# Keys and values of the linear heads: transposed by VectorE blocks and DMA instead of TensorE, and a new order of steps inside each head

## The chip, the cores and the metric

One core of a Trainium2 chip runs the whole kernel. The metric is the device time of one execution in microseconds (us), the median of three runs; lower is better. TensorE (PE) multiplies, VectorE (DVE) and ScalarE (ACT) work elementwise and read PSUM, GpSimd (POOL) works elementwise on SBUF and issues DMAs, SyncE (SP) only issues DMAs. Each engine has its own queue of instructions, run in order; engines meet through semaphores alone.

## The reference, cut to what matters

One layer over 576 tokens (512 of a prompt, 64 of a running stream), width 2048. One input projection gives the operands of three mixers (pooling, stick-breaking attention with 8 heads of 128, linear "mLSTM" heads, 4 of 256), their gates and three merge gates of width 2048. The linear heads are the part that changes:

```python
s = jnp.einsum('bhld,bhsd->bhls', qc, kc) * w_intra
num = jnp.einsum('bhls,bhsv->bhlv', s, vc) + w_inter[..., None] * jnp.einsum('bhlk,bhkv->bhlv', qc, c)
den = jnp.sum(s, axis=-1) + w_inter * jnp.einsum('bhlk,bhk->bhl', qc, n)
h_out = num / jnp.maximum(jnp.abs(den), jnp.exp(-m_t))[..., None]
...
c_new = decay[..., None, None] * c + jnp.einsum('bhs,bhsk,bhsv->bhkv', w_end, kc, vc)
...
h_ml = h_ml * lax.rsqrt(jnp.mean(h_ml * h_ml, axis=-1, keepdims=True) + RMS_EPS)
...
for bi, yb in enumerate((pool_y, sb_y, ml_y)):
    gated = yb * jax.nn.silu(cols(OFF_Z + bi * BRANCH_W, BRANCH_W))
    term = jax.nn.sigmoid(cols(...)) * jnp.einsum('btw,wd->btd', gated, w_branch[bi])
    merged = term if merged is None else merged + term
y = jnp.einsum('btd,de->bte', merged, w_out)
```

Scores `s` contract over the channels of keys and queries; the weighing `num` and the state `c_new` contract over tokens, so for them keys and values must lie with tokens on the partitions.

## The kernel before, in words

Everything is computed in fp32 quality out of fp32r matmuls: each operand is split into a high and a low part (`..._hi` made by ACT, `..._lo` by DVE as the rest), and three products are added.

**Input projection** (0 to about 1577 us). 68 pairs of column tiles, each by seven products of Strassen-Winograd form (`pair_products`, L1029). Activations lie with channels on the partitions and tokens along the row. The list `SPILLS` sets which group of columns each pair from the 3rd on computes: queries, keys and values of the attention heads (SQ, SK, SV), those of the linear heads (MQ, MK, MV), gates (MO, ZSB, ZML, G0 to G2). POOL stores each pair to `z_scratch` in HBM (`store_pair`). Pairs of a kind "turned" (SK, SV: eight pairs) are also transposed: DVE transposes all 32x32 blocks of the pair into `tokens` (`to_tokens`, L2264), and 16 DMAs of POOL put the blocks in their places in HBM (`store_tokens`). Every turned pair is followed by one of another kind.

**Attention heads** (1577 to 1742 us). A "segment" `seg(h, s)` is half of a tile of the branch projection: 24 matmuls that need the weights `wb_hi`, `wb_lo` and gated activations `gt_hi`, `gt_lo`. Segments are the filler that PE runs while DVE and ACT work on a head. `SB_SLOTS` says how many segments stand behind each of the steps scores, (middle of the scores), `weights_to_keys` and `weigh_values` of a head. After a tile DVE merges it with its gate (`merge`, L2485 or L2488 and L2491).

**Linear heads** (1742 to 1921 us). `ML_SLOTS` is the same for `ml_head`. Its steps on PE are, in order: KTR, ten transposes of keys from `ml_k` to the PSUM tensor `M` (L1047); SCORES (L1368); VTR, ten transposes of values from `ml_v`; WEIGH, numerator and denominator (L1347, L1390); SSQ, sums of squares by a matmul with ones (L1396); STATE, the new state (L1407). All steps share the four banks of `M`, so each waits until DVE or ACT has read the step before. Between the steps stand 2, 1, 1, 2, 1, 1 segments. On DVE and ACT each head has: `mk_hi`, `mk_lo` (keys times a decay, split); `decay_rows` (five instructions into `W_ml`, L2602), the exponential on ACT (L1844), a causal mask on POOL (L2985, four instructions), the product with the scores (L2655), the split `S_hi`, `S_lo` and the split of values `mv_hi`, `mv_lo`; copies of the numerator (L2676 to L2680); squares, `den`, a reciprocal (L2695), the gate (`gate`, L2630 and L2631), and `read_state`. The gated result of head 3 goes straight into `gt_hi`, `gt_lo` (`gated_hi_direct`, `gated_lo_direct`, L2538), those of the others through HBM.

**Rest** (1921 to 2223 us): the third branch's segments from `seg(H_ML, 0)` on, then the output projection.

SP issues all loads in one written order; each waits for its buffer to be free. The order of instructions on every engine is written out by hand.

Of the kernel before, what the change touches and what calls it, by code (L numbers as in the profile page):

```python
# [48 lines left out]
ZT_SQ, ZT_SK, ZT_MQ, ZT_MK, ZT_MV, ZT_MO, ZT_ZSB, ZT_ZML, ZT_G = 0, 8, 16, 24, 32, 40, 48, 56, 64  # L49
ZT = 112  # L50
SQ, SK, SV, MQ, MK, MV, MO, ZSB, ZML, G0, G1, G2 = range(12)
GROUP_COLUMN = [W, 2 * W, 3 * W, 4 * W, 5 * W, 6 * W, 7 * W, OFF_Z + W, OFF_Z + 2 * W, OFF_G, OFF_G + D, OFF_G + 2 * D]
GROUP_TILE = [ZT_SQ, ZT_SK, None, ZT_MQ, ZT_MK, ZT_MV, ZT_MO, ZT_ZSB, ZT_ZML, ZT_G, ZT_G + KD, ZT_G + 2 * KD]
TURNED = (SK, SV)
# [13 lines left out]
TURN_DMAS = 4 * TURN_PARTS  # L68
# [13 lines left out]
SB_SLOTS = [[1, 1, 1, 1]] * 3 + [[1, 1, 1, 0]] * 3  # L82
ML_SEGS = ([(16, 1), (17, 1)] + [(h, s) for h in range(H_SB + 2, H_ML - 2) for s in range(2)]
           + [(30, 0), (31, 0), (30, 1), (31, 1)])

ML_SLOTS = [[2, 1, 1, 2, 1, 1], [2, 1, 1, 2, 1, 1], [2, 1, 1, 1, 1, 1], [2, 1, 1, 2, 1, 0]]
# [123 lines left out]
def tokens_stored(n):  # L210

    return 16 * TURN_DMAS * n
# [84 lines left out]
def only_turned(p):  # L297

    return not is_pool(p) and SPILLS[spill_of(p)][0] == SV

# [11 lines left out]
def hybrid_layer(nc, x_prompt, x_sample, cache_sb_k, cache_sb_v, state_pool, state_ml_c, state_ml_n,  # L312
# [21 lines left out]
                  for pair in ((p_k, s_k), (p_v, s_v))]  # L334
    past_v_v = cache_sb_v.rearrange("a b t h d -> (a b t) (h d)")
# [15 lines left out]
    with ctx:  # L351
# [102 lines left out]
        states = sb("states", R + 82944, [P, 2 * MC * MDH])  # L454
# [11 lines left out]
        ml_v = sb("ml_v", R + 138240, [P, MC, T])  # L466
# [169 lines left out]

        g_ready, ghi_ready, glo_ready, g_stored = sem("g_ready"), sem("ghi_ready"), sem("glo_ready"), sem("g_stored")
# [21 lines left out]
        c0_loaded, mktr_done, mkhi_ready, kw_ready = sem("c0_loaded"), sem("mktr_done"), sem("mkhi_ready"), sem("kw_ready")  # L659
        D_ready, W_ready, Wm_ready = sem("D_ready"), sem("W_ready"), sem("Wm_ready")  # L660
        scores_done, sw_ready, mvtr_done, mvtok_ready = sem("scores_done"), sem("sw_ready"), sem("mvtr_done"), sem("mvtok_ready")
# [14 lines left out]
        def _(sp):  # L676
# [176 lines left out]
            for i in range(1, SBH):  # L853
# [10 lines left out]
                merge_gate(2 * i + 3)  # L864
                weights(2 * i + 4)
# [15 lines left out]

            def ml_v_in(i):
                if i:
                    sp.wait_ge(mvtr_done, i)
                sp.dma_start(ml_v[:, :, :], z_v[:, ZT_MV + MC * i:ZT_MV + MC * (i + 1), :]).then_inc(mv_loaded, 16)
# [24 lines left out]
            sp.wait_ge(at_done, SBH)  # L910
            ml_v_in(0)
            sp.wait_ge(av_done, SBH)
# [5 lines left out]
            for i in range(MLH):  # L918
# [10 lines left out]
                if more:  # L929
                    ml_v_in(i + 1)  # L930
                    ml_q_in(i + 1)
# [15 lines left out]
                if more:  # L947
                    ml_o(i + 1)
                    ml_c0(i + 1)
# [68 lines left out]
        def _(pe):  # L1018
# [243 lines left out]
            def scores(i, between=()):  # L1262
# [7 lines left out]
                for qb, col, w in SB_QUERIES:  # L1270
                    if col >= SB_BANK:
                        for h, s in between:
                            seg(h, s)
                        if i >= 2:
                            pe.wait_ge(g_ready, PG + i - 1)
                    nc.tensor.matmul(M[:, col:col + w], qT[:, qb * P:(qb + 1) * P], kT[:, 0:w], start=True, stop=True)  # L1276
# [5 lines left out]
            def weights_to_keys(i):  # L1282
# [4 lines left out]
                if i:  # L1287
                    pe.wait_ge(g_ready, PG + i)
# [7 lines left out]
            def weigh_values(i):  # L1296
                pe.wait_ge(at_read, i + 1)
                pe.wait_ge(v_loaded[i % 2], 32 * (i // 2 + 1))
# [22 lines left out]
            for i in range(2, SBH):  # L1321
                scores(i, sb_segs(i, 0))
                for h, s in sb_segs(i, 1):
                    seg(h, s)
                weights_to_keys(i - 1)
                for h, s in sb_segs(i, 2):
                    seg(h, s)
                weigh_values(i - 1)
                for h, s in sb_segs(i, 3):
                    seg(h, s)  # L1330
# [6 lines left out]
            seg(H_SB, 0)  # L1337
            seg(H_SB + 1, 0)
# [11 lines left out]
            def ml_head(i):  # L1350
                pe.wait_ge(mk_loaded, 16 * (i + 1))
                if i:
                    pe.wait_ge(state_ready, i + 1)
                else:
                    pe.wait_ge(at_read, SBH)
                for blocks in (range(NT), [NT]):
                    if not i and blocks[0]:
                        pe.wait_ge(g_ready, PG + SBH)
# [3 lines left out]
                for h, s in ml_segs(i, 0):  # L1362
                    seg(h, s)
                pe.wait_ge(kw_ready, i + 1)
                pe.wait_ge(mq_loaded, 16 * (i + 1))
# [5 lines left out]
                for h, s in ml_segs(i, 1):  # L1371
                    seg(h, s)
                pe.wait_ge(sw_ready, i + 1)
                pe.wait_ge(mv_loaded, 16 * (i + 1))
                transposes([(M[:, MDH * j + P * c:MDH * j + P * (c + 1)], ml_v[:, c, TOKEN0[j]:TOKEN0[j] + P])
                            for j in range(NB) for c in range(MC)]).then_inc(mvtr_done, 1)
                for h, s in ml_segs(i, 2):
                    seg(h, s)
# [13 lines left out]
                for h, s in ml_segs(i, 3):  # L1392
                    seg(h, s)
                for b in range(2):
                    pe.wait_ge(squares_ready, 2 * i + b + 1)
                    m = nc.tensor.matmul(M[:, 512 * b:512 * b + TH], ones[:, :], W_ml[:, b * TH:(b + 1) * TH],  # L1396
                                         start=True, stop=True)
                m.then_inc(ssq_done, 1)
                for h, s in ml_segs(i, 4):
                    seg(h, s)  # L1400
                pe.wait_ge(ssq_read, i + 1)
# [8 lines left out]
                for h, s in ml_segs(i, 5):  # L1410
# [132 lines left out]
        def _(act):  # L1543
# [289 lines left out]

            def ml_head(i):
                h = H_SB + 4 * i
                act.wait_ge(mktr_done, i + 1)
                if i:
                    act.wait_ge(state_done, i)
                for kb in range(NB):
                    k = nc.scalar.activation(mk_hi[:, kb, :], M[:, MDH * kb:MDH * (kb + 1)], ACT.Copy,  # L1840
                                             scale=wend[:, i, kb:kb + 1])
                k.then_inc(mkhi_ready, 1)
                act.wait_ge(D_ready, i + 1)
                nc.scalar.activation(W_ml[:, :], W_ml[:, :], ACT.Exp, scale=-1.0).then_inc(W_ready, 1)  # L1844
                split_hi(At(h + 2))
                act.wait_ge(sw_ready, i + 1)
# [3 lines left out]
                act.wait_ge(mvtr_done, i + 1)  # L1850
# [1356 lines left out]
```

## Time and profile before

| | before |
|---|---|
| median of 3 runs | 2224.07 us (2224.0 to 2224.45) |
| profiled execution: its time | 2225.11 us |
| profiled execution: span from first to last instruction | 2223.3 us |
| PE busy | 2208.7 us (99%) |
| DVE busy | 1539.5 us (69%) |
| ACT busy | 947.2 us (43%) |
| POOL busy | 234.8 us (11%) |
| granted TensorE clock | 0.999 |
| DMA, mean | 143 GB/s |

The span leaves out about 1.8 us around it. "Busy" of PE counts modelled ends of pipelined matmuls; how far apart the starts of two groups lie says what a group costs. In the chain of work that ended last PE has 96%.

### The profile page before, as it was taken

Reading aid. Unit: us, or ns where it says so; the run is one execution under the profiler, and the core shown is the slowest. Engines: PE = TensorE matmul, PEld = TensorE weight load, DVE = VectorE, ACT = ScalarE, POOL = GpSimd, SP = SyncE. Lnnn points to the kernel's source line nnn. Section 1 sums busy time; section 2 is a strip of 40 time slices with the busy share of each in tenths; the row PEclk is TensorE's granted clock in tenths of the full one; section 3 lists DMA queues with packets and bytes.
Section 4 is the critical chain, followed back from the end, with each engine's and each line's share of the span. In section 5 each row is a group of like instructions: output and inputs, shape, how many; then the busy total and the mean of one; then the engine's idle time right before and its main releaser. Section 6 shows DMA issues by size and latency. Waiting matters only on the chain.

```text
span 2223.3 us, 38578 instructions
## 1 busy us (share of the span) xinstructions
PE 2208.7 (99%) x16186; PEld 2163.9 (97%) x16186; DVE 1539.5 (69%) x1788; ACT 947.2 (43%) x1280; POOL 234.8 (11%) x335
## 2 busy tenths in 40 slices
PE   9999999999999999999999999999999999999998
PEld 7999999999999999999999999999988999999998
DVE  7876768657666667676676666666577577778676
ACT  5343434334444444434444444444555234324543
POOL 0000000000100023323320000000001112100000
PEclk9999999999999999999999999999999999999999
DMA  6444453534444445454545343444765765763448
GB/s 181 116 128 110 111 144 103 150 105 124 122 117 123 131 130 145 122 143 102 142 109 136 108 133 111 129 116 135 236 210 151 250 194 175 189 169 90 130 131 270
DMA packets 426060, 318.04 MB, mean 143 GB/s; under 512 B 13325, under 2 KB 386965, under 8 KB 424480
## 3 DMA queue, kind: packets, MB, share of 16 engines
q1 hardware_dynamic: 403520, 251.18, 41.0%
q0 software_dynamic: 22288, 63.87, 9.2%
q8 instruction: 129, 2.11, 0.4%
q10 hardware_dynamic: 80, 0.52, 0.1%
q14 instruction: 43, 0.35, 0.0%
HBM read 254.53 MB, written 60.99 MB: 142 GB/s over the span
## 4 chain that ended last, share of the span: by engine, by line
PE 96%; DVE 1%; DMA 1%; ACT 1%; issue 0%; POOL 0%; SPq 0%; DVEq 0%; POOLq 0%; ACTq 0%
PE pp L1029 67%; PE pp L1255 12%; PE pp L1431 7%; PE M L1047 2%; PE pp L1039 1%; PE M L1347 1%; PE pp L1528 1%; PE M L1216 1%; PE M L1039 1%; PE M L1368 1%; PE M L1276 1%; PE M L1301 1%; DMA gt_lo<-gated_scratch 1%; PE M L1407 0%; PE pp L1514 0%
## 5 line engine op out<-in xcount | busy, mean ns | idle before, releaser
L1029 PE MATMUL pp<-xa,wa_hi 128*128 128x288 f32 x7392 | 1480.3, 296 | 0.1
L1029 PEld LDWEIGHTS pp<-xa,wa_hi 128*128 128x128 f32 x7392 | 1185.5, 188 | 1.1 <-DVE zs L2170 0.4
L1029 PE MATMUL pp<-xa,wa_lo 128*128 128x288 f32 x3696 | 1086.7, 294 | 0.0
L1029 PEld LDWEIGHTS pp<-xa,wa_lo 128*128 128x128 f32 x3696 | 696.1, 188 | 0.0
L2058 DVE TENSOR_TENSOR wa_lo<-raw_a,wa_hi 128x1024 fp32r<-128x1024 f32 x262 | 319.3, 1221 | 223.5 <-ACT wa_hi L1550 223.4
L1550 ACT ACTIVATE wa_hi<-raw_a 128x1024 fp32r<-128x1024 f32 x262 | 276.7, 1056 | 204.8 <-PE pp L1029 203.8
L2058 DVE TENSOR_TENSOR wa_lo<-raw_r,wa_hi 128x1024 fp32r<-128x1024 f32 x134 | 177.2, 1322 | 147.8 <-ACT wa_hi L1550 147.8
L1550 ACT ACTIVATE wa_hi<-raw_r 128x1024 fp32r<-128x1024 f32 x134 | 141.4, 1055 | 134.0 <-PE pp L1029 126.7
L1255 PE MATMUL pp<-gt_hi,wb_hi 128*128 128x288 f32 x768 | 169.1, 302 | 0.7 <-DMA gt_lo<-gated_scratch 0.7
L1255 PE MATMUL pp<-gt_hi,wb_lo 128*128 128x288 f32 x768 | 164.3, 295 | 0.0
L1255 PE MATMUL pp<-gt_lo,wb_hi 128*128 128x288 f32 x768 | 164.3, 295 | 0.0
L3038 POOL DMA_DIRECT2D z_scratch<-zs x56 | 40.6, 725 | 966.4 <-ACT zs L1689 590.3
L2062 DVE TENSOR_TENSOR raw_a<-raw_a 128x1024 f32<-128x1024 f32 x111 | 135.2, 1218 | 0.0
L2058 DVE TENSOR_TENSOR wa_lo<-tx_main,wa_hi 128x1024 fp32r<-128x1024 f32 x67 | 82.1, 1225 | 67.3 <-ACT wa_hi L1550 67.3
L1255 PEld LDWEIGHTS pp<-gt_hi,wb_hi 128*128 128x128 f32 x768 | 122.9, 189 | 3.0 <-issue 0.9
L1255 PEld LDWEIGHTS pp<-gt_hi,wb_lo 128*128 128x128 f32 x768 | 123.5, 188 | 0.0
L1255 PEld LDWEIGHTS pp<-gt_lo,wb_hi 128*128 128x128 f32 x768 | 123.5, 188 | 0.0
L1614 ACT ACTIVATE s<-pp 128x288 f32<-128x288 f32 x67 | 27.6, 412 | 150.6 <-PE pp L1029 150.6
L1431 PE MATMUL pp<-s,oa_hi 128*128 128x288 f32 x448 | 89.8, 295 | 0.0
L3016 POOL DMA_DIRECT2D out_dram<-tokens x128 | 75.7, 600 | 90.9 <-DVE tokens L2264 89.8
L1608 ACT ACTIVATE s<-pp 128x288 f32<-128x288 f32 x67 | 27.6, 412 | 134.8 <-PE pp L1029 134.8
L1666 ACT ACTIVATE zs<-pp 128x288 f32<-128x288 f32 (+2 forms) x71 | 27.8, 398 | 134.1 <-PE pp L1029 132.0
(368 smaller groups left out, 2568.5 us busy)
## 6 DMA issues: line engine op xcount, KB each, us to landing
raw_a<-in_w_in_dram SPq DMA_DIRECT2D x202, 512.0 KB, 5.1
raw_r<-in_w_in_dram SPq DMA_DIRECT2D x68, 512.0 KB, 5.1
z_scratch<-zs POOLq DMA_DIRECT2D x56, 576.0 KB, 3.3
raw_b<-in_w_branch_dram SPq DMA_DIRECT2D x48, 512.0 KB, 4.3
gz<-z_scratch SPq DMA_DIRECT2D x48, 288.0 KB, 4.3
raw_a<-in_w_out_dram SPq DMA_DIRECT2D x20, 512.0 KB, 6.4
gt_hi<-gated_scratch SPq DMA_DIRECT2D x4, 1152.0 KB, 7.4
gt_lo<-gated_scratch SPq DMA_DIRECT2D x4, 1152.0 KB, 10.5
```

What stands on the lines that cost most here:

```text
L1029: i = nc.tensor.matmul(out, ws[:, slot, k, :], xa[:, o, part, k, :], start=opens and k == 0 and s == 0, stop=k == HK - 1 and s == 2, skip_ ...
L1039: i = nc.tensor.matmul(out, weights[:, k, :], x[:, k, :], start=opens and k == 0, stop=k == HK - 1, skip_group_check=not opens)
L1047: i = nc.tensor.transpose(out, src, ident[0:k, 0:k])
L1255: i = nc.tensor.matmul(out[:, b, :], ws[:, slot, k, :], xs_[:, k, b * TH:(b + 1) * TH], start=k == 0 and q == 0, stop=k == HK - 1 and q == 2)
L1431: i = nc.tensor.matmul(out, ws[m % 3][:, k, :], xs_[:, k, :], start=opens and k == 0 and s == 0, stop=k == HK - 1 and s == 2, skip_group_c ...
L1550: nc.scalar.activation(wa_hi[:, ring(n), :, :], src, ACT.Copy).then_inc(wa_hi_ready, 1)
L1608: nc.scalar.activation(s1[:, :], a_of(p), ACT.Copy).then_inc(s1_ready, 1)
L1666: i = nc.scalar.activation(dst, a_of(p)[:, lo:hi_], ACT.Copy)
L2058: nc.vector.tensor_tensor(wa_lo[:, ring(n), :, :], src, wa_hi[:, ring(n), :, :].bitcast(F32), ALU.subtract).then_inc(wa_lo_ready, 1)
L2062: nc.vector.tensor_tensor(out, a, b, ALU.subtract).then_inc(t_ready, 1)
L3016: pool.dma_start(turned_out[TURNED.index(group)][out][:, :, 2 * j + n, i, :], src[:, n, t0:t1].rearrange("p (j c) -> p j c", c=TURN)).then ...
L3038: pool.dma_start(z_v[:, at:at + 2, :], staged_pair(p)).then_inc(stored, 16)
```

## The change

Keys and values of the linear heads join the turned groups; they are put with tokens on the rows into two new HBM tensors `kt_scratch` and `vt_scratch` by 8 DMAs a pair, and are loaded from there straight into `mk_lo` and `mv_lo`, from which ACT and DVE split them. The pairs are put in another order. The twenty PE transposes of each linear head go; what is left is SCORES, WEIGH, STATE, SSQ. `decay_rows` of the next head stands right behind the reciprocal, ahead of `gate`; `states` has a buffer of its own beside `W_ml`. In the attention heads the segments stand in two groups a head, and the sample part of the gate has a semaphore of its own.

```diff
-TURNED = (SK, SV)
+TURNED = (SK, SV, MK, MV)
-SPILLS = members(SQ) + members(MQ) + members(MK) + members(MV) + members(G0, 0, 8) + members(G1, 0, 1)
-for to_turn, plain in zip(members(SK) + members(SV), members(ZSB) + members(ZML)):
+SPILLS = members(SQ) + members(G0, 0, 7) + members(MQ) + members(G0, 7, 8) + members(G1, 0, 8) + members(G2, 0, 1)
+for to_turn, plain in zip(members(SK) + members(SV) + members(MK) + members(MV),
+                          members(ZSB) + members(ZML) + members(MO) + members(G2, 1, 5)):
     SPILLS += [to_turn, plain]
-SPILLS += members(G1, 1, 8) + members(MO) + members(G2, 0, 8)
+SPILLS += members(G2, 5, 8)
-SB_SLOTS = [[1, 1, 1, 1]] * 3 + [[1, 1, 1, 0]] * 3
+SB_SLOTS = [[2, 2]] * 3 + [[2, 1]] * 3
-ML_SLOTS = [[2, 1, 1, 2, 1, 1], [2, 1, 1, 2, 1, 1], [2, 1, 1, 1, 1, 1], [2, 1, 1, 2, 1, 0]]
+SCORES, WEIGH, STATE, SSQ = range(4)
+ML_SLOTS = [[4, 2, 2, 1], [3, 2, 2, 1], [3, 2, 2, 1], [3, 2, 2, 0]]
...
+            def ml_tokens(i, dst, src, loaded):
+                if i:
+                    sp.wait_ge(state_done, i)
+                else:
+                    sp.wait_ge(av_done, SBH)
+                cols = src[:, i * MDH:(i + 1) * MDH]
+                sp.dma_start(dst[:, 0:NT, 0:MDH].bitcast(F32), cols[0:TP, :].rearrange("(m p) c -> p m c", p=P)).then_inc(loaded, 16)
+                sp.dma_start(dst[:, NT, 0:MDH].bitcast(F32), cols[T - P:T, :]).then_inc(loaded, 16)
...
             sp.wait_ge(z_done, SBH)
             ml_q_in(0)
+            head_past_v(SBH - 1)
+            merge_gate(2 * SBH + 1)
+            weights(2 * SBH + 2)
+            ml_k_in(0)
             ml_gate_rows(0)
-            ml_k_in(0)
-            head_past_v(SBH - 1)
...
                 if more:
                     ml_o(i + 1)
+                    ml_v_in(i + 1)
+                    ml_kt_in(i + 1)
                     ml_c0(i + 1)
...
+                pe.wait_ge(mq_loaded, 16 * (i + 1))
                 if i:
-                    pe.wait_ge(state_ready, i + 1)
+                    pe.wait_ge(ssq_read, i)
...
-                    m = transposes([(M[:, MDH * j + P * c:MDH * j + P * (c + 1)], ml_k[:, c, TOKEN0[j]:TOKEN0[j] + P])
-                                    for j in blocks for c in range(MC)])
-                m.then_inc(mktr_done, 1)
...
-                transposes([(M[:, MDH * j + P * c:MDH * j + P * (c + 1)], ml_v[:, c, TOKEN0[j]:TOKEN0[j] + P])
-                            for j in range(NB) for c in range(MC)]).then_inc(mvtr_done, 1)
...
-                act.wait_ge(mvtr_done, i + 1)
-                nc.scalar.activation(mv_hi[:, :, 0:MDH], M[:, 0:NB * MDH].rearrange("p (j d) -> p j d", j=NB), ACT.Copy
+                act.wait_ge(mv_loaded, 32 * (i + 1))
+                nc.scalar.activation(mv_hi[:, :, 0:MDH], mv_lo[:, :, 0:MDH].bitcast(F32), ACT.Copy).then_inc(mvhi_ready, 1)
                 act.wait_ge(sw_ready, i + 1)
...
-                    decay_rows(i)
+                    decay_rows(0)
+                else:
                     gated_lo(PG + SBH + MC * (i - 1), zml[:, 0, :])
-                    merges(i - 1, STATE)
+                    merges(i - 1, SSQ)
...
                 steps.link(nc.vector.reciprocal(den[:, :], den[:, :]))
-                merges(i, SSQ)
                 if i < MLH - 1:
-                    read_state(i)
+                    decay_rows(i + 1)
                 gate(i)
```

PE's queue at the second linear head. Before, from the last segment ahead of the keys' transposes to the weighing (`M` is PSUM, `pp<-gt..` are segments, left out between the rows):

```order
L1047 MATMUL M<-ident,ml_k 128x128 [waits state_ready,mk_loaded]
L1047 MATMUL M<-ident,ml_k 128x128 x9
L1255 MATMUL pp<-gt_hi,wb_hi 128x288 [waits psum_read,wb_lo_ready]
...
L1368 MATMUL M<-ml_q,ml_k 128x512 [waits mq_loaded,kw_ready]
...
L1047 MATMUL M<-ident,ml_v 128x128 [waits mv_loaded,sw_ready]
L1047 MATMUL M<-ident,ml_v 128x128 x9
...
L1347 MATMUL M<-S_hi,mv_hi 128x512 [waits c0_loaded,mvtok_ready,slo_ready]
```

The same stretch now, from the sums of squares of the head ahead:

```order
L1409 MATMUL M<-W_ml,ones 128x288 [waits squares_ready,state_ready]
L1409 MATMUL M<-W_ml,ones 128x288 [waits squares_ready]
...
L1374 MATMUL M<-ml_q,ml_k 128x512 [waits ssq_read,mq_loaded,mk_loaded]
L1374 MATMUL M<-ml_q,ml_k 128x512
...
L1361 MATMUL M<-S_hi,mv_hi 128x512 [waits c0_loaded,mvtok_ready,slo_ready]
```

The transposes and their waits are gone, and between the sums of squares of one head and the weighing of the next PE has one segment, the scores and three segments.

DVE's queue from the reciprocal of a head to the weighing of the next. Before:

```order
L2695 RECIPROCAL den<-den 128x576 [waits norm_act]
L2617 COPY states<-M 128x512 [waits state_done,dve_steps]
...
L2631 SCALAR_TENSOR_TENSOR zml<-num,hnorm,zml 128x576 [waits dve_steps]
L2643 SCALAR_TENSOR_TENSOR mk_lo<-M,wend,mk_hi 128x256 [waits state_done,mkhi_ready]
L2643 SCALAR_TENSOR_TENSOR mk_lo<-M,wend,mk_hi 128x256 x4
L2602 TENSOR_SCALAR W_ml<-G_h,acol 128x512 [waits state_stored,ssq_done,mrow_loaded]
...
L2655 SCALAR_TENSOR_TENSOR W_ml<-M,W_ml 128x1344 [waits Wm_ready,scores_done]
```

Now:

```order
L2602 TENSOR_SCALAR W_ml<-G_h,acol 128x512 [waits ssq_done,mrow_loaded,dve_steps]
...
L2630 TENSOR_TENSOR num<-num,den 128x576 [waits zg_ready]
L2631 SCALAR_TENSOR_TENSOR zml<-num,hnorm,zml 128x576 [waits dve_steps]
L2630 TENSOR_TENSOR num<-num,den 128x576
L2631 SCALAR_TENSOR_TENSOR zml<-num,hnorm,zml 128x576 [waits dve_steps]
L2539 TENSOR_TENSOR g_lo<-zml,g_hi 128x576 [waits ghi_ready]
L2480 TENSOR_TENSOR wb_lo<-raw_b,wb_hi 128x1024 [waits wb_hi_ready]
L2645 SCALAR_TENSOR_TENSOR W_ml<-M,W_ml 128x1344 [waits Wm_ready,scores_done]
```

`decay_rows` moved ahead of the gate, the state is read before the reciprocal, and `mk_lo` stands behind the weighing's operands.

## Rows read from the trace of the kernel before

**Rows 1.** The page, part 1: busy us (share) xinstructions.

```profile
PE 2208.7 (99%) x16186; PEld 2163.9 (97%) x16186; DVE 1539.5 (69%) x1788; ACT 947.2 (43%) x1280; POOL 234.8 (11%) x335
```

**Rows 2.** Waits of PE: waited for, us in total, times, longest.

```profile
PE M L1396 <- DVE W_ml L2683: 0.8, 1, 0.8
PE M L1301 <- DMA past_v<-in_cache_sb_v_dram: 0.7, 1, 0.7
PE pp L1255 <- DMA gt_lo<-gated_scratch: 0.7, 1, 0.7
```

**Rows 3.** Timeline of PE, second linear head: start us, us, instruction, xcount.

```profile
1792.79 1.25 PE L1047 MATMUL M<-ident,ml_k 128*128 128x128 f32 x10
1793.80 0.51 PE L1255 MATMUL pp<-gt_hi,wb_hi 128*128 128x288 f32 x2
...
1800.27 4.87 PE L1368 MATMUL M<-ml_q,ml_k 128*128 128x512 f32 x20
1804.95 0.51 PE L1255 MATMUL pp<-gt_hi,wb_hi 128*128 128x288 f32 x2
...
1808.21 1.25 PE L1047 MATMUL M<-ident,ml_v 128*128 128x128 f32 x10
```

**Rows 4.** Timeline of PE: first head's sums of squares; third head's with a wait.

```profile
1781.83 1.13 PE L1396 MATMUL M<-W_ml,ones 128*128 128x288 f32 x4
1782.58 0.64 PE L1255 MATMUL pp<-gt_hi,wb_hi 128*128 128x288 f32 x2
...
1785.99 0.28 PE L1407 MATMUL M<-mv_hi,mk_hi 128*128 128x258 f32 x1
...
1867.14 0.43 PE L1255 MATMUL pp<-gt_hi,wb_lo 128*128 128x288 f32 x2
1868.34 0.51 PE L1396 MATMUL M<-W_ml,ones 128*128 128x288 f32 x1 [0.77 <-DVE W_ml L2683]
```

**Rows 5.** Timeline of DVE, first to second linear head.

```profile
1785.00 3.75 DVE L2695 RECIPROCAL den<-den 128x576 f32<-128x576 f32 x1 [0.75 <-ACT den L1868]
...
1798.01 1.43 DVE L2602 TENSOR_SCALAR W_ml<-G_h,acol 128x512 f32<-128x512 f32 x5
...
1801.77 1.23 DVE L2476 TENSOR_TENSOR wb_lo<-raw_b,wb_hi 128x1024 fp32r<-128x1024 f32 x1 [0.21 <-ACT wb_hi L1782]
...
1805.17 1.56 DVE L2655 SCALAR_TENSOR_TENSOR W_ml<-M,W_ml 128x1344 f32<-128x1344 f32 x1 [0.56 <-PE M L1368]
...
1808.13 1.56 DVE L2664 TENSOR_TENSOR S_lo<-W_ml,S_hi 128x1344 fp32r<-128x1344 f32 x1 [0.74 <-ACT S_hi L1849]
```

**Rows 6.** Timelines of ACT and POOL there: exponential, mask; mask of the fourth head.

```profile
1799.47 1.33 ACT L1844 ACTIVATE W_ml<-W_ml 128x1344 f32<-128x1344 f32 x1 [2.16 <-DVE W_ml L2602]
...
1800.88 3.91 POOL L2985 TENSOR_TENSOR W_ml<-W_ml,mask 128x128 f32<-128x128 f32 x4 [7.03 <-ACT W_ml L1844]
...
1889.52 0.87 POOL L2985 TENSOR_TENSOR W_ml<-W_ml,mask 128x128 f32<-128x128 f32 x2 [8.22 <-ACT W_ml L1844]
```

**Rows 7.** Timelines of POOL and DVE in the second head: two instructions at once.

```profile
1821.93 2.69 POOL L3132 TENSOR_TENSOR zml<-zml,oml 128x1152 f32<-128x1152 f32 x1 [6.11 <-DMA zml<-z_scratch]
...
1822.23 3.08 DVE L2683 TENSOR_TENSOR W_ml<-W_ml 128x288 f32<-128x288 f32 x2
```

**Rows 8.** Timeline of DVE, last linear head: gate and direct split.

```profile
1921.77 0.75 DVE L2630 TENSOR_TENSOR num<-num,den 128x576 f32<-128x576 f32 x1
...
1924.82 1.59 DVE L2538 TENSOR_TENSOR gt_lo<-zml,gt_hi 128x576 fp32r<-128x576 f32 x2
```

**Rows 9.** Timeline of DVE, an attention head: the sample part of the gate.

```profile
1671.40 0.22 DVE L2529 TENSOR_TENSOR zsb<-M,zsb 128x64 f32<-128x64 f32 x1
```

**Rows 10.** DVE's block transposes; their stretch: us, busy PE, PEld, DVE, ACT, POOL.

```profile
L2264 DVE STREAM_TRANSPOSE tokens<-zs x8: 1372/1372/1372, 825.2 to 1138.8; 128x1152 f32<-128x1152 f32 x8
...
825.00:1150.00 325.00, 325.00 (x2440) 325.00 (x2439) 225.66 (x211) 133.53 (x167) 102.55 (x146) 1.00 0.49 129
```

**Rows 11.** The tile `ml_v`: its loads.

```profile
DMA to landing us min/median/max: 6.2/7.9/8.8
```

More of the change, by code:

```diff
@@ L297, in only_turned @@
 def only_turned(p):
-    return not is_pool(p) and SPILLS[spill_of(p)][0] == SV
+    return not is_pool(p) and SPILLS[spill_of(p)][0] in (SV, MV)
 def stored_before(p):
@@ L1260, in seg, with scores @@
                     i.then_inc(gt_free, 1)
-            def scores(i, between=()):
+            def scores(i):
                 pe.wait_ge(kq_loaded[i % 2], 32 * (i // 2 + 1))
@@ L1391, in ml_head @@
                 m.then_inc(num_done, 1)
-                for h, s in ml_segs(i, 3):
+                for h, s in ml_segs(i, WEIGH):
                     seg(h, s)
[L1394 to L1401, printed above, removed]
+                pe.wait_ge(num_ready, 3 * (i + 1))
+                pe.wait_ge(kw_ready, i + 1)
                 for c in range(MC):
@@ L1409, in ml_head @@
                 m.then_inc(state_done, 1)
-                for h, s in ml_segs(i, 5):
+                for h, s in ml_segs(i, STATE):
+                    seg(h, s)
+                pe.wait_ge(state_ready, i + 2)
+                for b in range(2):
+                    pe.wait_ge(squares_ready, 2 * i + b + 1)
+                    m = nc.tensor.matmul(M[:, 512 * b:512 * b + TH], ones[:, :], W_ml[:, b * TH:(b + 1) * TH],
+                                         start=True, stop=True)
+                m.then_inc(ssq_done, 1)
+                for h, s in ml_segs(i, SSQ):
                     seg(h, s)
@@ L1832, in _, with decay_exp @@
             gated_hi_direct(PG + SBH - 1, H_SB, SBH - 1, zsb[1][:, :])
+            def decay_exp(i):
+                act.wait_ge(D_ready, i + 1)
+                nc.scalar.activation(W_ml[:, :], W_ml[:, :], ACT.Exp, scale=-1.0).then_inc(W_ready, 1)
             def ml_head(i):
                 h = H_SB + 4 * i
[L1836 to L1844, printed above, removed]
+                if not i:
+                    decay_exp(0)
                 split_hi(At(h + 2))
+                act.wait_ge(mv_loaded, 32 * (i + 1))
+                nc.scalar.activation(mv_hi[:, :, 0:MDH], mv_lo[:, :, 0:MDH].bitcast(F32), ACT.Copy).then_inc(mvhi_ready, 1)
                 act.wait_ge(sw_ready, i + 1)
@@ L1856, in ml_head @@
                     gated_hi(PG + SBH + k, PG + SB_STORED + k, zml[:, 1, :])
+                act.wait_ge(mkt_loaded, 32 * (i + 1))
+                for kb in range(NB):
+                    k = nc.scalar.activation(mk_hi[:, kb, :], mk_lo[:, kb, :].bitcast(F32), ACT.Copy,
+                                             scale=wend[:, i, kb:kb + 1])
+                k.then_inc(mkhi_ready, 1)
                 split_hi(At(h + 4))
@@ L2565, in _ @@
                 logits(i)
-                for h in sb_halves(i, 0):
-                    merge(h)
                 gated_lo(PG + i - 2, zsb[i % 2][:, :])
@@ L2670, in ml_head @@
                     gated_lo(PG + SBH + MC * (i - 1) + 1, zml[:, 1, :])
-                merges(i, SCORES, VTR)
+                merges(i, SCORES)
+                dve.wait_ge(mkhi_ready, i + 1)
+                for kb in range(NB):
+                    last = nc.vector.scalar_tensor_tensor(mk_lo[:, kb, :], mk_lo[:, kb, :].bitcast(F32),
+                                                          wend[:, i, kb:kb + 1], mk_hi[:, kb, :].bitcast(F32),
+                                                          ALU.mult, ALU.subtract)
+                last.then_inc(kw_ready, 1)
                 split_lo(At(h + 4))
```

120 lines of the change are left out of this document (50 added, 70 removed).

## The prediction

> **What bounds the kernel now.** I read the page first. PE is busy for 2208.7 us of a span of 2223.3, DVE for 69% of it [rows 1]; so the time is PE's work plus the few gaps in it. Next the waits of PE: behind the start-up none is over 0.8 us, and those in the heads are three [rows 2] and one of 0.2 us. What DVE, ACT and the DMAs do is hidden, as long as nothing that PE needs comes later than now. Two questions follow: how much PE work goes, and whether a wait appears where none was. For the first the distance between starts on PE's timeline counts, not the duration of an instruction, because matmuls overlap.
>
> **PE work removed.** Ten transposes take 1.25 us as a group but hold PE for 1793.80 - 1792.79 = 1.01 us [rows 3]. A segment alone between two groups takes 1808.21 - 1804.95 = 3.26 us, two in a row take 1800.27 - 1793.80 = 6.47, so the second of them 3.21: an interruption costs some 0.06 more. There are two such groups a head, those of values like those of keys: 8 x (1.01 + 0.06) = 8.6 us. The trace shows a transpose of 272 ns; the Trainium skill (TensorE: Matmul & The Clock Gate, Part 4: PE-mode transpose) gives about 275 ns for one, measured in a kernel. That agrees as a duration, but eighty of them priced so would be 22 us, and the rows of starts forbid it: I take 8.6.
>
> **Waits removed.** The three of [rows 2] and the 0.2 us are 2.4 us by the waits' own account. In starts they are larger: the sums of squares of the third head start 1868.34 - 1867.14 - 0.27 = 0.93 us late where the wait is given as 0.77 [rows 4]; four times 0.15 makes 3.0 us. All four should go: `past_v` is now asked for before merge gates and weights; the gated activations of the second branch (`gt_lo`) are now needed after the first scores, 4.7 us later; the sums of squares stand four segments and the state behind the weighing, where that head had one segment; the values no longer wait for the scores' product.
>
> **SB heads, edits of nothing.** Segments in two groups instead of four save interruptions, but the scores run unsplit and directly behind `weigh_values`; by the starts of both forms this cancels to 0.2 us more in all. A new closeness: scores of columns from 1024 on wait for the sample gate, right after the values. The gate itself is short, 0.22 us [rows 9], but stands behind DVE's exponents and a merge; in the last heads it comes, by my sum of the same instructions in the new order, 1.5 us after the scores' start, and is needed at 1.7. Nothing, with 0.2 us to spare.
>
> **Projection, edit of nothing.** Eight more block transposes of 1.37 us on DVE. Their cover: in the 325 us with the eight transposes of now DVE was busy 225.7 and PE all of the 325.00 [rows 10]; the new ones stand in pairs without POOL's silu product, so with less work than these. POOL's 8 DMAs a pair replace no wait of anyone. Uncovered it would cost up to 1.37 us each.
>
> **New wait 1: the weighing of heads 1 to 3.** Let 0 be the start of a head's sums of squares on PE. PE then has 0.75 and one segment of 3.41 [rows 4], the next scores, 1804.95 - 1800.27 = 4.68 [rows 3], and three segments, 6.47 + 3.21 = 9.68; it wants the weighing at 18.5. The other side is now one chain:
> - the reciprocal starts at 1785.00 - 1781.83 = 3.2 and ends at 6.9 [rows 4, 5];
> - `decay_rows` 1.43, to 8.4 [rows 5]; exponential 1.33, to 9.75; the mask on POOL starts at 9.8 [rows 6];
> - DVE meanwhile has four gate instructions, 3.05 us from start to start of what follows [rows 8], from 8.3 to 11.4, then `g_lo`, one more instruction of 576 columns like the gate's at a quarter of 3.05, and `wb_lo` 1.23 less the overlap of about 0.1 [rows 5]: free at 13.2;
> - from the scores' product to the end of `S_lo` are 1808.13 + 1.56 - 1805.17 = 4.5 us [rows 5], and `mv_lo`, 1280 columns against the 1344 of `S_lo` in 1.56, adds 1.4: 5.95 with the semaphore.
>
> With DVE free at 13.2 the weighing would start at 19.2, 0.7 us late. But mask and DVE disturb each other. POOL worked from 1821.93 to 1824.62, and two short additions of DVE, begun in between, ended at 1825.30, 0.7 us after POOL [rows 7]: DVE had stood still. The mask has 576 columns, of which the first 256 took 0.87 us [rows 6], so some 1.9 us undisturbed; in the second head it took 3.91 beside DVE's work. The four instructions of DVE that now run beside it (two of the gate, `g_lo`, `wb_lo`) all read two SBUF operands, without a pause between them. The delay of DVE lies between nothing (`wb_lo` kept its 1.23 us beside the mask, though it had idle time around it [rows 5]) and 1.9. I take 1.1, a little over the middle, since DVE has no idle time left to absorb it: 13.2 + 1.1 = 14.3, the weighing at 20.3, 1.8 us late, three times: **5.4 us**. The Trainium skill (SBUF — State Buffer, the section on the shared port) says the pair of ports is a lock held for the whole instruction and the loser blocks fully; by that the whole 1.9 us add up, a rival below. The first head has four segments here and I expect no wait.
>
> **New wait 2: the third branch's start.** The last head's result goes straight into `gt_lo`. Before, segment, state and two segments lay between its sums of squares and the first use; now only two segments and the first half of a third. With the same zero: gate from 6.95; 1924.82 - 1921.77 + 0.75 = 3.8 us later the first tile is there [rows 8], at 10.75. PE: 0.75 + 3.41 + 3.21 + 1.60 (half a segment) = 8.97. **1.8 us** late; the second tile follows 0.8 later, in step with PE.
>
> **Values by DMA.** ACT's `S_hi` now stands behind `mv_hi`, which waits for the load. SP issues it at about 3; `ml_v`'s loads landed in 6.2 to 8.8 us [rows 11], so at 12 at the latest, `mv_hi` is done by 13.3, `S_hi` wanted at 15.9: covered, with 2.6 us spare. The states' own buffer and the earlier state cost nothing: the state's wait for the copied numerators lies two segments behind the weighing.
>
> **Sum.** -8.6 - 3.0 + 0.2 + 5.4 + 1.8 = -4.2 us. The profiled execution's time was 2225.11, 1.0 above the median of the runs, and I take the difference over to the median: 2224.07 - 4.2 = 2219.9, rounded **2220.0 us**. 0.2% of this kernel, about what a measurement can tell from no change, is 4.45 us, so this is within it, at its edge.
>
> **The rivals.**
> - *No collision*: mask and gate pass each other, product at 13.2, wait 0.7 x 3 = 2.1. -7.4, 2216.7 us. For: the mask may finish in DVE's gaps. Against: rows 6 and 7. Chance 0.25.
> - *Full collision*: each of the four holds DVE for its whole length, or waits until DVE has emptied; product at 15.1, wait 2.6 x 3 = 7.8. -1.7, 2222.4 us. For: DVE's additions that stood still. Against: the second head, where DVE's `wb_lo` kept its 1.23 us beside the mask [rows 5]. Chance 0.2.
> - *Slower*: the turned pairs stop PE in the projection. It decides where DVE reaches its split of weights more than the slack of a ring of three late. Each of the eight then costs up to 1.37 us: 11.0, giving 2231 us. Against: PE's 325.00 of 325 with the same pattern [rows 10]. Chance 0.08.
> - My forecast has 0.42; 0.05 is for what I don't see, a load that comes late at the first linear head, for one.
>
> **How the numbers follow.** Faster by over 0.2% (under 2219.6): the first rival and 0.17 of my own case, whose start of the product is uncertain by half a microsecond, three times: 0.42. Slower by over 0.2%: 0.10. Same: 0.48. The range reaches from just under the first rival, 2216.0, to above the second, 2224.5.
>
> **What would show it.** In the profile after: no matmul on `ident,ml_k` or `ident,ml_v`; PE waits at the weighing three times, between 0.7 and 2.6 us, put down to `mv_lo`; one wait of about 2 us in a segment for `gt_lo` from DVE; the mask at 3 to 5 us; no PE wait in the projection, with sixteen block transposes; the waits of rows 2 gone. A wait at the attention heads' scores, at the state, or in the projection would prove me wrong, and a weighing that waits for nothing would prove the chain wrong.

## The result, and the profile after

The changed kernel takes **2230.99 us** (median of 12 runs, 2229.46 to 2232.81), the kernel before 2224.65 (12 runs): a ratio of 1.0026, 95% interval 1.0018 to 1.0034. It is slower by 0.26%, or 6.3 us; the forecast was 2220.0, with 2216.0 to 2224.5 as its range. The profiled execution has a span of 2229.2 us. (Three executions in all, one of run 9, one of run 10 and one of the kernel before beside them, took 4351 to 11341 us and are left out of every median.) Part 1 of its page, to be read against [rows 1]:

```profile
PE 2203.4 (99%) x16106; PEld 2158.6 (97%) x16106; DVE 1556.6 (70%) x1796; ACT 947.7 (43%) x1280; POOL 279.9 (13%) x395
```

The eighty transposes are gone from PE, whose busy time fell by 5.3 us, while the span grew by 5.9. So some 11 us of idle time are new. The waits of PE from the end of the projection to the output, all of them (waited for, us in total, times, longest); they answer to [rows 2]:

```profile
PE pp L1273 <- DMA gt_lo<-gated_scratch: 7.3, 1, 7.3
PE M L1361 <- issue: 5.4, 3, 1.8
```

The three waits of [rows 2] are gone. Three of 1.8 us stand at the weighing (L1361), as forecast. One of 7.3 us is new: the third branch waits for a load that no term of the forecast mentions. On PE's timeline:

```profile
1914.92 1.13 PE L1409 MATMUL M<-W_ml,ones 128*128 128x288 f32 x4
1915.68 0.64 PE L1273 MATMUL pp<-gt_hi,wb_hi 128*128 128x288 f32 x2
...
1929.73 0.85 PE L1273 MATMUL pp<-gt_hi,wb_hi 128*128 128x288 f32 x2 [7.28 <-DMA gt_lo<-gated_scratch]
1931.34 0.68 PE L1273 MATMUL pp<-gt_hi,wb_hi 128*128 128x288 f32 x2
...
1935.35 0.43 PE L1273 MATMUL pp<-gt_hi,wb_hi 128*128 128x288 f32 x2
1936.14 0.43 PE L1273 MATMUL pp<-gt_hi,wb_hi 128*128 128x288 f32 x2
```

The third branch starts at 1915.68. In the kernel before it started behind the last state:

```profile
1921.12 0.43 PE L1255 MATMUL pp<-gt_hi,wb_hi 128*128 128x288 f32 x2
```

Up to here the change has **gained 5.4 us**. Then two segments, and PE stands until 1929.73. It goes on slowly: from 1929.73 to 1935.35 four tiles of the activations (six matmuls each), 1.41 us each, then 0.79. The four cost 2.4 us more than at full speed. The windows of that stretch (us, busy time of PE, PEld, DVE, ACT, POOL, then granted clock, share of the DMAs, GB/s) show the reason for both:

```profile
1916.00:1920.00 4.00, 4.00 (x32) 4.00 (x31) 3.25 (x3) 0.69 (x1) 0.00 (x0) 1.00 0.95 22
1920.00:1924.00 4.00, 2.45 (x19) 2.22 (x17) 3.93 (x4) 0.47 (x1) 0.00 (x0) 1.00 0.61 31
...
1926.00:1930.00 4.00, 0.27 (x1) 0.28 (x2) 1.76 (x2) 0.69 (x1) 0.00 (x0) 0.50 1.04 349
1930.00:1935.00 5.00, 5.00 (x22) 5.00 (x23) 0.00 (x0) 1.06 (x1) 0.00 (x0) 0.51 0.60 178
1935.00:1940.00 5.00, 5.00 (x40) 5.00 (x39) 3.89 (x5) 1.06 (x1) 0.00 (x0) 1.00 0.25 72
```

The granted clock is 0.50 (1.2 GHz) from 1926 to 1935, after PE had stood idle, and 1.00 again from 1935. And from 1916 to 1924 the DMAs were busy 0.95 and 0.61 of the time and moved 22 and 31 GB/s. What they had in hand shows on the timelines of POOL and SP:

```profile
1911.23 0.76 POOL L3135 DMA_DIRECT2D out_dram<-states  x1 [6.09 <-DVE states L2622]
1912.20 0.72 POOL L3135 DMA_DIRECT2D out_dram<-states  x1 [0.21 <-issue]
1912.92 0.90 POOL L3140 DMA_DIRECT2D out_dram<-n_out  x1
1913.81 0.88 POOL L3141 DMA_DIRECT2D out_dram<-n_out  x1
...
1915.12 0.36 SPq L767 DMA_DIRECT2D gt_hi<-gated_scratch  x1
1915.52 0.47 SPq L767 DMA_DIRECT2D gt_lo<-gated_scratch  x1
```

`n_out` is 128 partitions by 8 floats for each of two outputs, and the floats of one partition lie apart in DRAM: 4 KB in writes of 4 bytes, twice. Its stores are issued when the last head's state is read. Before, the state was the last step of a head, and they went out at 1930.3:

```profile
1930.29 0.91 POOL L3141 DMA_DIRECT2D out_dram<-n_out  x1
```

Now it stands ahead of the sums of squares, they go out at 1912.9, and 2.2 us behind the first of them comes the load of the gated activations for the third branch's second halves. From the list of DMA issues in this stretch (KB each, us to landing):

```profile
gt_hi<-gated_scratch SPq DMA_DIRECT2D x1, 576.0 KB, 12.8
gt_lo<-gated_scratch SPq DMA_DIRECT2D x1, 576.0 KB, 14.2
out_dram<-states POOLq DMA_DIRECT2D x1, 256.0 KB, 3.2
out_dram<-n_out POOLq DMA_DIRECT2D x2, 4.0 KB, 11.6
```

The same two loads in the kernel before, where no `n_out` store was on its way:

```profile
gt_hi<-gated_scratch SPq DMA_DIRECT2D x1, 576.0 KB, 4.3
gt_lo<-gated_scratch SPq DMA_DIRECT2D x1, 576.0 KB, 5.5
```

The slow stretch is in the kernel before too, 20 us later, where PE wanted nothing from DRAM within it; its window:

```profile
1935.00:1943.00 8.00, 8.00 (x62) 8.00 (x62) 1.08 (x2) 1.26 (x2) 0.00 (x0) 1.00 0.69 36
```

In the projection nothing happened. The sixteen block transposes, and PE's busy time over the stretch with the new ones, against [rows 10]:

```profile
L2268 DVE STREAM_TRANSPOSE tokens<-zs 128x1152 f32<-128x1152 f32 x16 | 22.0, 1372 | 0.0
...
1150.00:1500.00 350.00, 350.00 (x2627) 350.00 (x2627) 235.10 (x228) 143.93 (x181) 49.78 (x72) 1.00 0.48 126
```

### The profile page after: what moved, and what is told of

The parts are those of the page before. It is cut to its first block, busy times and chain, and to the rows that moved or that the text cites. A ratio compares the mean times of both kernels' runs of the same rounds, so it can differ in the third digit from the quotient of the medians.

```text
span 2229.2 us, 38514 instructions
## 1 busy us (share of the span) xinstructions
PE 2203.4 (99%) x16106; PEld 2158.6 (97%) x16106; DVE 1556.6 (70%) x1796; ACT 947.7 (43%) x1280; POOL 279.9 (13%) x395
## 4 chain that ended last, share of the span: by engine, by line
PE 96%; DVE 2%; DMA 1%; POOL 1%; ACT 0%; issue 0%; DVEq 0%; SPq 0%
PE pp L1047 66%; PE pp L1273 12%; PE pp L1433 7%; PE M L1065 1%; PE pp L1057 1%; PE M L1361 1%; PE M L1292 1%; PE pp L1530 1%; PE M L1319 1%; PE M L1234 1%; PE M L1057 1%; PE M L1401 1%; DMA gt_lo<-gated_scratch 1%; POOL W_ml L2981 1%; DVE den L2693 1%; PE pp L1516 0%
```

## Experiments

Theory A: the `n_out` stores hold up the load issued behind them. Theory B: the load is late for another reason, its nearness to other transfers or to its use. The first two runs take the stores away from the load, and put them ahead of it where they were not. All times are medians beside runs of the kernel before on the same chip (2224.5 us in the first four, 2225.5 in the next four, 2224.7 in the last two). The change itself and each of these three groups were measured apart, and the kernel before moved by 1 us between them; where two runs of different groups are compared, PE's timeline is given as well.

### 1. The stores held back, in the kernel after

```
+            pool.wait_ge(gt_loaded[1], 32 * 3)
             pool.dma_start(p_n_v, n_out[:, 0, :], allow_slow_non_contiguous=True).then_inc(n_stored, 16)
```

> The kernel after, with one wait more on POOL: the two stores of n_out (writes of 4 bytes each) are issued only when the second half of the third branch's gated activations has landed. Theory A, these stores hold up the load: after them the DMAs moved 15 to 50 GB/s for 9 us, in the trace after (1915.5 to 1924.5) as in the trace before (1935 to 1943). Then the load, issued at 1915.5, lands in some 8.8 us as before, PE waits 1.9 us in place of 7.3 and most of the 4 to 5 us at the lower clock behind it goes: 2231.0 - 5.4 - 2.6 = 2223.0 us. Theory B, the load is late because it is issued closer to the other loads and stores (states, weights) and PE now wants it 7.3 us behind the last segment in place of 9.8: the wait stays at 5 to 7 us, 2229 to 2231 us.

Measured: **2221.92 us**, ratio 0.9987 (0.9978 to 0.9996). The waits of PE in the same stretch as above:

```profile
PE M L1361 <- issue: 5.3, 3, 1.8
PE pp L1273 <- DVE gt_lo L2543: 1.7, 1, 1.7
```

The load's wait is gone, the state's stores stayed where they were, and 9.1 us came back, 8.2 of them on PE's timeline between the last sums of squares and a group of transposes of `yT` near the end (289.65 in the kernel after, 281.48 here). The profiled execution of this run is its slowest, 2225.7 us; it lost its time behind these transposes, where it took 27.4 us to the end and the other profiles 23.6 to 24.9. What is left is the wait of 1.7 us for DVE's direct tile, which the forecast had at 1.8. The expectation was off in the load's time: it landed in 5.1 us, not 8.8 (that was the other load of `gt_lo`, twice the size), so it ends nobody's wait.

### 2. The stores put ahead of the load, in the kernel before

```
                 nc.gpsimd.tensor_tensor(zml[:, :, :], zml[:, :, :], oml[:, :, :], ALU.mult).then_inc(zg_ready, 1)
+                if i == MLH - 1:
+                    pool.wait_ge(wb_used, H_ML - 1)
+                    store_n(0, MC * (MLH - 1))
```

`store_n` stores the named columns of `n_out` to both outputs; the last head's two columns follow at the end.

> The kernel before, with the n_out columns of the first three linear heads (three quarters of the 4-byte writes) stored when segment 31 of the second branch is next, some 4 us ahead of the issue of the same load, and the last head's at the end as now. Theory A: they keep the DMAs at a few tens of GB/s for three quarters of 9 us, the load lands 3 to 6 us later than 1926.9 and PE, which wants it at 1927.5, waits 2 to 5 us and restarts at the lower clock: 2228 to 2232 us. Theory B: the tiny stores are harmless, no new wait, 2224.7 us.

Measured: **2230.34 us**, ratio 1.0023 (1.0014 to 1.0033). PE waits 3.5 us at the third branch (its waits), for a load that took 13.9 us (the tile `gt_lo` there):

```profile
PE pp L1255 <- DMA gt_lo<-gated_scratch: 3.5, 1, 3.5
```

```profile
DMA to landing us min/median/max: 13.9/13.9/13.9
```

The tiles behind the wait ran at a lower clock here too (granted 0.57 over 1923 to 1927). Nothing of the change is in this kernel but the place of 6 KB of stores, and it is as slow as the changed one. Theory B is out.

### 3 and 4. A segment moved ahead of the weighing

```
-ML_SLOTS = [[4, 2, 2, 1], [3, 2, 2, 1], [3, 2, 2, 1], [3, 2, 2, 0]]
+ML_SLOTS = [[4, 2, 2, 1], [4, 2, 1, 1], [4, 2, 1, 1], [4, 2, 1, 0]]
```

> The kernel after, with one segment moved from behind the state to ahead of the weighing in heads 2 to 4. The weighing then is wanted 3.2 us later than now, 1.4 us after its operands are there. Theory: the three waits of 1.8 us go, and with them 1.6 us that the first of them costs in a restart at the lower clock; the third branch's wait is untouched: 2231.0 - 5.4 - 1.6 = 2224.0 us. Rival: the chain is paced by the sums of squares of the head before, which also come 3.2 us earlier relative to the segments, or a new wait appears at them (one segment less behind the state): 2229 to 2231 us.

> Both edits, of the held stores and of the moved segments. If the two causes are independent their gains add: 2231.0 - 8.0 - 7.0 = 2216.0 us, with one wait of some 2 us at the third branch left. If theory B holds, 2224; if the slots move the wait elsewhere, 2223.

Measured: **2238.13 us** (1.0041 to 1.0075) alone and **2236.79 us** (1.0032 to 1.0066) with the held stores. Both expectations failed. The weighing waits no more, but PE waits longer elsewhere (run 3):

```profile
PE pp L1273 <- DVE gz L2492: 14.7, 3, 5.2
```

The fourth segment writes the bank of PSUM that the merge of a segment before must have read, and that merge stood in DVE's list behind all the splits for the weighing. In the second head of the kernel after DVE read it at 1803.85, where a fourth segment would have stood at 1799.5: DVE had been late for it all along; with three segments nobody asked. Run 3 has no wait for the load, though its stores were not held: its state was read later, the stores went out at 1928.86, 0.6 us behind the load (1928.26), which then landed in 6.0 us. Hence so little between the two runs, and a question for run 10.

### 5. The merge put behind the scores' product

```
                                                ).then_inc(sw_ready, 1)
+                early = ml_halves(i, (SCORES,))[:1] if i else []
+                for m in early:
+                    merge(m)
```

and out of its old place; the rest as in run 4.

> The held stores, the moved segment, and DVE's merge of the segment before, which stood behind the splits of weights and values, put directly behind the scores' product. In the run with the moved segment alone PE waited three times 4.3 to 5.2 us for that merge (gz), because the fourth segment needs its bank. Theory: the merge's first instruction ends some 0.8 us behind the product, at 15.9 to 16.8 us from the start of the sums of squares, before the fourth segment at 18.5; the weighing's operands are there at some 21.1 and are wanted at 21.7: no wait in heads 2 to 4, 2221.9 - 5.4 - 1.6 = 2215.0 us, and only the 1.7 us for the direct tile left. Rival: the merge lengthens DVE's chain by its full 1.5 us and more, the weighing waits 0.5 to 1.5 us again: 2217 to 2220 us.

Measured: **2216.48 us**, ratio 0.9957 (0.9942 to 0.9972), 5.4 us under run 1. The weighing waits nowhere, and one wait is left from the projection's end to the output, the 1.7 us for DVE's `gt_lo` as in run 1.

On PE's timeline the stretch from the first head's sums of squares to the fourth's went from 134.16 us in run 1 to 126.56. These 7.6 us are the 5.3 of the three waits, 1.6 that the second head's weighing ran slowly in run 1, and 0.7 more. Against run 6, which has the same waits and no slow weighing, it is 132.57 - 126.56 = 6.0.

### 6 and 7. The third branch's second halves interleaved

```
-            seg(H_ML, 1)
-            seg(H_ML + 1, 1)
+            for ks in (range(2), range(2, 4)):
+                for h in (H_ML, H_ML + 1):
+                    seg(h, 1, ks)
```

> The held stores, and at the third branch's start the first two tiles of the second halves of segments 32 and 33 ahead of the last two of both, so that the tiles that come straight from the last head are wanted 1.6 us later. With the stores held PE waited 1.7 us for DVE's gt_lo there. Theory: that wait falls to 0.1 or nothing, 2221.9 - 1.6 = 2220.3 us. Rival: the load of the second half, which landed 8 us behind its issue and is wanted as early as before, is now the one that ends the wait: no gain, 2221.9.

> Held stores, moved segment with its merge, and the third branch's second halves interleaved. If the causes are independent: 2221.9 - 7.0 - 1.6 = 2213.3 us, and no PE wait over 0.3 us between the start-up and the output.

Measured: **2221.04 us** (0.9970 to 0.9990) with the held stores alone, and **2213.49 us** (0.9929 to 0.9958) with everything. In the profile of either PE waits for no `gt_lo`; in run 7 it waits for nothing from the projection's end to the output. Between the last head's sums of squares and a group of transposes of `yT` near the end lie 2196.41 - 1914.93 = 281.48 us in run 1 and 2193.97 - 1913.66 = 280.31 in run 6; in runs 5 and 7 it is 281.51 (2189.33 - 1907.82) and 280.25 (2187.57 - 1907.32). The wait was 1.7 us and its removal is worth **1.2**; the medians (0.9 and 3.0) scatter too much to tell.

Run 6 showed something else. From the first head's sums of squares to the third's it took 1869.50 - 1781.09 = 88.4 us, in run 1 it took 1870.72 - 1780.77 = 89.95, with the same waits at the weighing. In run 1, as in the kernel after, the second head's weighing ran slowly behind its wait (granted clock 0.83 over 1800 to 1810), in run 6 at 1.00. No other head of the three showed it.

### 8. Three of the mask's four blocks left out

The mask is multiplied into one of its four blocks in heads 2 to 4; otherwise run 1.

```
-                apply_mask(W_ml, ML_MASKED).then_inc(Wm_ready, 1)
+                apply_mask(W_ml, ML_MASKED[:1] if i else ML_MASKED).then_inc(Wm_ready, 1)
```

> The held stores, and in heads 2 to 4 the mask multiplied into one of its four blocks only (the other three are left out, which changes what is computed). Theory, mask and gate lengthen each other: the mask takes some 1 us in place of 4.5, DVE is free some 0.9 us earlier (its six instructions beside the mask went from 4.9 us in the rows of before to 5.8 after), and the weighing waits 0.7 to 0.9 us in place of 1.8: 2221.9 - 3 = 2219 us. Rival, the port costs nothing and DVE's own list sets the time: the wait stays at 1.5 to 1.8 us, 2221.9.

Measured: **2217.70 us**, ratio 0.9962 (0.9947 to 0.9977), 4.2 us under run 1. DVE's timeline in the second head of the kernel after, with the whole mask beside it:

```profile
1789.16 0.75 DVE L2630 TENSOR_TENSOR num<-num,den 128x576 f32<-128x576 f32 x1
...
1792.30 1.01 DVE L2539 TENSOR_TENSOR g_lo<-zml,g_hi 128x576 fp32r<-128x576 f32 x1
1793.23 1.76 DVE L2480 TENSOR_TENSOR wb_lo<-raw_b,wb_hi 128x1024 fp32r<-128x1024 f32 x1
1795.28 1.56 DVE L2645 SCALAR_TENSOR_TENSOR W_ml<-M,W_ml 128x1344 f32<-128x1344 f32 x1 [0.29 <-POOL W_ml L2981]
```

and with one block of it:

```profile
1790.06 0.75 DVE L2630 TENSOR_TENSOR num<-num,den 128x576 f32<-128x576 f32 x1
...
1793.19 0.74 DVE L2539 TENSOR_TENSOR g_lo<-zml,g_hi 128x576 fp32r<-128x576 f32 x1
1793.86 1.21 DVE L2480 TENSOR_TENSOR wb_lo<-raw_b,wb_hi 128x1024 fp32r<-128x1024 f32 x1
1794.99 1.54 DVE L2645 SCALAR_TENSOR_TENSOR W_ml<-M,W_ml 128x1344 f32<-128x1344 f32 x1
```

From the first gate instruction to the scores' product are 6.12 us with the whole mask and 4.93 with one block: 1.2 us, of which 0.8 are `g_lo` and `wb_lo`, longer by 0.27 and 0.55, and 0.3 is a wait for the mask itself. The mask took 4.47 us for its four blocks, where rows 6 give some 1.9 undisturbed (an estimate). PE's waits at the weighing fell from 5.3 to 1.8 us in all. From the first sums of squares to the fourth's PE took 129.01 us: 3.6 less than in run 6, and 5.2 less than in run 1, which had the slow weighing too. The collision is real, and here both sides lengthen.

### 9. The transposes put back

Twenty transposes of `ml_k` and `ml_q` per head, ahead of the scores and unused, in the kernel of run 7.

```
+                for src in (ml_k, ml_q):
+                    transposes([(M[:, MDH * j + P * c:MDH * j + P * (c + 1)], src[:, c, TOKEN0[j]:TOKEN0[j] + P])
+                                for j in range(NB) for c in range(MC)])
```

> The fastest kernel so far (held stores, moved segment with its merge, interleaved second halves) with twenty transposes put back ahead of each linear head's scores (results unused), as many as the change took away. Theory: they hold PE for 1.01 us per ten and nothing hides them, so the heads' period grows from 42.2 to 44.2 us: 2213.5 + 8.1 = 2221.6 us, up to 2222.1 with the interruptions. Rival: part of the removed transposes' time was slack that other engines used, a wait goes as they come back: 2216 to 2219 us.

Measured: **2222.92 us** (0.9981 to 1.0001), 9.4 us over run 7. PE's timeline:

```profile
1831.38 1.25 PE L1065 MATMUL M<-ident,ml_k 128*128 128x128 f32 x10
1832.47 1.25 PE L1065 MATMUL M<-ident,ml_q 128*128 128x128 f32 x10
1833.56 1.88 PE L1377 MATMUL M<-ml_q,ml_k 128*128 128x512 f32 x4
```

From the second head's sums of squares to the third's are 1871.55 - 1827.22 = 44.33 us, in run 7 they are 1865.13 - 1822.94 = 42.19: 2.14 for this head. The last head's start at 1915.94 in place of 1907.32, 8.62 later, with all eighty in front.

### 10. The kernel of run 7 without the held stores

> The same fastest kernel with the two stores of n_out issued at once again. They would then be issued some 1 us behind the load of the third branch's second halves, in the kernel after they were 2 us ahead of it. Theory A, the 4-byte writes hold up whatever shares the DMAs with them, also what was issued just before: the load lands late and PE waits 2 to 6 us at the third branch, 2216 to 2220 us. Rival: only transfers issued behind them suffer: 2213.5 us.

Measured: **2214.22 us** (0.9930 to 0.9970), the same as run 7 within the scatter; from the last sums of squares to the transposes of `yT` PE took 279.88 us, in run 7 280.25. The time of the rival came out. The stores were issued at 1908.86 and 1909.75, the load's second part at 1908.25, and it landed in 5.9 us. But the rival's reason, that only what is issued behind the stores suffers, does not hold. The load of weights issued next, at 1908.79, is still 0.07 us ahead of the first store (KB each, us to landing):

```profile
gt_lo<-gated_scratch SPq DMA_DIRECT2D x1, 576.0 KB, 5.9
raw_b<-in_w_branch_dram SPq DMA_DIRECT2D x1, 512.0 KB, 15.1
```

In run 7, where the stores went out at 1914.06, that load was issued at 1908.46, and the load of `gz` behind it at 1909.10, five microseconds ahead of the stores:

```profile
raw_b<-in_w_branch_dram SPq DMA_DIRECT2D x1, 512.0 KB, 8.7
gz<-z_scratch SPq DMA_DIRECT2D x1, 288.0 KB, 15.6
```

A `gz` load usually lands in 4.4 us (median of 29 in the kernel before, 1600 to 1900). In run 10 the DMAs slow down only at about 1915 (182 GB/s over 1914 to 1915, 34 over the next microsecond), just after the load of `gt_lo` had landed at 1914.2. So what fits all of these is that the stores delay what has not landed when the slow stretch begins, whether it was issued behind them or a little ahead. PE waited for none of the late loads here.

## Why the prediction was wrong

The step that failed is the last sentence of "Values by DMA": **"The states' own buffer and the earlier state cost nothing"**. With it "New wait 2", the third branch's start, had the wrong wait: it priced 1.8 us for DVE's direct tile, and PE waited 7.28 for a load. I asked only whether the state itself was wanted too soon. The state carries stores with it, and these were moved 17 us earlier, past the issue of a load that PE needs. I had listed SP's queue for the values and not POOL's for the last head's stores. The miss against the forecast, worked out on PE's timeline: the third branch's wait was 7.28 us for 1.8, 5.5 more, and the tiles behind it cost 2.4 us at the lower clock. With the 1.6 us of the slow weighing of the second head (6.97 us from 1801.30 to 1808.27, 5.36 to 5.40 in the other heads) that makes 9.5, of the 11.0 between forecast and result; run 1 gave back 9.1 (8.2 on PE's timeline) by the one wait on POOL. The rest are small things: some 0.7 more in the third branch, 1.0 behind the last transposes of `yT` (24.6 us to the end, before 23.6), and 0.9 because the profiled execution of the kernel before stood 1.0 above its median and that of the changed kernel did not; against them the other terms up to the third branch came out 1 us better than forecast.

The other steps, one by one:
- *PE work removed, -8.6*: right. Run 9 measured 8.6 on PE's timeline (9.4 in the medians). By the figure of the Trainium skill (TensorE: Matmul & The Clock Gate, Part 4: PE-mode transpose), about 275 ns each, the estimate would have been 22; start distances hold.
- *Waits removed, -3.0*: right as far as it shows; none of the four is there. (A fifth wait, 0.2 us for `qk`, was left out of the count; it is gone too, but stands with 0.3 to 0.6 us in runs 6, 8 and 10.) With the other terms up to the third branch's start, -8.6 - 3.0 + 0.2 + 5.4 = -6.0, and -4.4 with the 1.6 us of the slow weighing; the timeline has -5.4, so they were 1 us too small in all.
- *Attention heads*: no new wait, as said.
- *Projection, nothing*: right. PE was busy for all of 350.00 us with the new transposes. The rival "slower" gave 2231 us and the result is 2231.0, but that is chance: not one microsecond was lost where it put them.
- *New wait 1, 5.4*: right to a tenth, 3 x 1.78. The product started 1795.28 - 1780.85 = 14.4 after the sums of squares, forecast 14.3; run 8 priced the collision at 1.2 us, where I took 1.1. That was a choice between nothing and 1.9, so being this near is partly luck. What I had not seen is that the mask itself ends last, by 0.3 us, and that a wait can cost more than its length: the sum had nothing for the lower clock, and the second head's slow weighing added 1.6. The Trainium skill (SBUF — State Buffer, "SBUF: two separate sides") has the loser block for the other's whole instruction; by that, and with DVE the loser each time, the estimate was 1.9 us of delay and waits of 2.6. The rows show 1.2 and 1.8, and a mask that took 4.47 us for its 1.9, so POOL lost more time than DVE; a lock for each instruction is not ruled out by this.
- *New wait 2, 1.8*: 1.7 in run 1, where nothing hides it.
- *Sum*: with the stores out of the way the kernel takes 2221.9, or 2.6 under the kernel before in the same runs (interval 0.9 to 4.9), forecast 4.2 under.

The Trainium skill (DMA: Bandwidth & Descriptors, Specifications) says that a transfer below 512 bytes misses line rate and becomes a read-modify-write. It says too (the same page, "Issuing engines are not separate DMA queues") that DMAs issued by different engines run on the same sixteen. The traces agree as far as they show it: 22 to 36 GB/s for some 8 us, and loads issued by SP that took 13.9 and 14.2 us instead of 5.5 beside stores issued by POOL. No run shows the read-modify-write itself. Neither rule says what runs 7 and 10 point to, that a load is safe if it lands before the slow stretch begins. Why 8 KB slow the DMAs for 8 us was not tried, nor was another layout of `n_out`: that the stores delay the load is shown (runs 1 and 2), by what means is open.

## What to carry to other kernels

When a step is moved, list every instruction it triggers downstream, stores to outputs included, and look where each lands among the loads that something is waiting for: here 8 KB of scattered writes cost about as much (8.2 us on PE's timeline, 9.1 in the medians) as eighty transposes had brought (8.6 and 9.4). A gain of PE time only counts up to the next thing that was just in time; after each edit read the waits again, since the next one is often an order in another engine's list (the merge in run 3) and costs one moved line. A time that matches a rival proves nothing about it; the place of the lost time does.

The best version found is run 7: the change, with the `n_out` stores held, a segment and its merge moved, and the third branch's second halves interleaved. It takes 2213.5 us, 0.56% under the kernel before (ratio 0.9944) and 17.5 us under the change. With the rest in place holding the stores gains nothing that can be told (run 10, 2214.2 us).

## What was not expected of the hardware

- Behind stores of 8 KB in 4-byte pieces the DMAs moved 22 to 36 GB/s for some 8 us, in the kernel before, after and in run 2; loads of 576 KB issued 2.6 and 4.3 us behind the first of them took 14.2 and 13.9 us instead of 5.5. A load issued 0.6 us ahead and landed before the slow stretch took 5.9.
- It is not that the stores' own transfers fill the DMAs. In run 1 the two stores were issued at 1920.89 and 1921.78 and landed in 9.3 us, and a `gz` load issued at 1916.71 took 15.1; while they were all outstanding, the DMAs' records show next to nothing (the last two numbers: share, GB/s):

```profile
1924.00:1930.00 6.00, 4.31 (x33) 4.24 (x32) 5.66 (x8) 2.80 (x4) 0.00 (x0) 1.00 0.01 1
```

- SP's issues were longer too: that of a `gz` load at 1916.70 took 4.08 us, where most take 0.33 to 0.66, and one in run 2 took 3.46; behind the held stores of run 1 two took 2.65 and 2.04. That the stores are the cause is not shown: in the same kernel one at 1578.46, with no such store about, took 2.26. The row is SP's timeline in the kernel after:

```profile
1916.70 4.08 SPq L760 DMA_DIRECT2D gz<-z_scratch  x1
```

- After 7.3 us without work PE ran at 1.2 GHz for 5.3 us, until 1935. After 1.8 us it ran slowly for some 3.5 us in the second head of two profiles (clock 0.83 over ten microseconds), and did not in the second head of run 6 and in the other heads.
